# Query transfers of the sliding-window items: whole token tiles of four head pairs, or halves of two

## The reference, cut to what matters

```python
u = _rmsnorm(h, g_pre[i])
qa, ka, va, za, qf, kf, vf, zf, ff, ga, gf = jnp.split(u @ w_in[i], split_idx, axis=-1)
y_swa = _swa_branch(qa, ka, va, sinks[i]) * jax.nn.silu(za)     # 8 query heads, 2 key heads
y_fox = _fox_branch(qf, kf, vf, log_f) * jax.nn.silu(zf)         # 8 heads, causal, 1040 keys
merged = (sigmoid(ga + b) * (y_swa @ w_up_swa[i])
          + sigmoid(gf + b) * (y_fox @ w_up_fox[i]))
h = h + _rmsnorm(merged @ w_out[i], g_post[i])
```

## Time and profile before

| | us |
|---|---|
| median of 3 runs | 817.27 |
| lowest, highest | 816.62, 818.16 |
| profiled execution, device time | 817.68 |
| its span, first to last instruction | 815.9 |

### The profile page before, as it was taken

How to read it: one execution, slowest core, us unless ns; L and a number is a source line. 1 busy time by engine, 2 the same in 40 slices (tenths; PEclk the granted TensorE clock), 3 DMA queues, 4 the chain that set the end, 5 groups by cost and what they waited for, 6 DMA issues and landing times.

```text
span 815.9 us, 12313 instructions
## 1 busy us (share of the span) xinstructions
PE 793.1 (97%) x4270; PEld 638.0 (78%) x4270; DVE 491.9 (60%) x1021; ACT 316.5 (39%) x650; POOL 339.5 (42%) x287
## 2 busy tenths in 40 slices
PE   6999999999999999999999999999998999999996
PEld 4999999988888888888888865656554788878885
DVE  6845788366777867745646466677777644442222
ACT  6532241333334323333333337666767122231111
POOL 1112213454535544444444425758766244412221
PEclk9999999999999999999999999999999999999999
DMA  9342424459855435344344599999700665352222
GB/s 279 105 129 56 131 66 115 126 162 240 205 132 162 109 96 143 110 116 124 102 130 119 137 250 241 243 241 219 184 1 22 208 185 154 104 206 78 103 78 78
DMA packets 127863, 116.05 MB, mean 142 GB/s; under 512 B 29741, under 2 KB 102269, under 8 KB 127802
## 3 DMA queue, kind: packets, MB, share of 16 engines
q1 hardware_dynamic: 126504, 111.53, 51.2%
q10 hardware_dynamic: 1298, 3.74, 1.2%
HBM read 81.99 MB, written 34.96 MB: 143 GB/s over the span
## 4 chain that ended last, share of the span: by engine, by line
PE 79%; DVE 5%; issue 4%; POOL 4%; SPq 3%; DMA 2%; ACT 2%; DVEq 0%; ACTq 0%; POOLq 0%
PE PS L1912 19%; PE PS L1913 19%; PE PS L1914 19%; PE PS L2174 4%; PE PS L2176 4%; PE PS L2175 4%; PE PS L2035 2%; POOL acc L1259 2%; DVE t_val L1648 2%; PE PS L2096 2%; DMA QBs<-q_swa_dram 1%; POOL w_plain L1211 1%; PE PS L2111 1%; PE PS L2127 1%; PE PS L2076 1%
## 5 line engine op out<-in xcount | busy, mean ns | idle before, releaser
L1190 POOL TENSOR_TENSOR ops<-s_sum,ops 128x512 fp32r<-128x512 f32 x64 | 89.1, 1401 | 106.6 <-ACT ops L1288 106.6
L1912 PE MATMUL PS<-t_hi,ops 128*128 128x512 f32 x256 | 100.1, 391 | 0.0
L1914 PE MATMUL PS<-t_hi,ops 128*128 128x512 f32 x256 | 99.9, 390 | 0.0
L1913 PE MATMUL PS<-t_lo,ops 128*128 128x512 f32 x256 | 99.9, 390 | 0.0
L1190 POOL TENSOR_TENSOR ops<-raw,ops 128x512 fp32r<-128x512 f32 x48 | 65.8, 1371 | 64.4 <-ACT ops L1288 64.0
L1211 POOL TENSOR_TENSOR w_plain<-raw,w_plain 128x1024 fp32r<-128x1024 f32 x10 | 27.7, 2769 | 100.7 <-ACT w_plain L1317 100.7
L1259 POOL TENSOR_TENSOR acc<-acc,p_fox 128x400 f32<-128x400 f32 (+5 forms) x76 | 61.4, 828 | 6.9 <-ACT p_fox L1416 5.8
L1730 DVE TENSOR_TENSOR z_tmp<-u,PS 128x512 f32<-128x512 f32 x48 | 33.0, 687 | 45.7 <-PE PS L1914 26.5
L1288 ACT ACTIVATE ops<-s_sum 128x512 fp32r<-128x512 f32 x64 | 39.6, 623 | 52.6 <-DVE s_sum L1524 46.8
L1416 ACT ACTIVATE p_fox<-PS,neg_c_col 128x512 f32<-128x512 f32 (+5 forms) x112 | 54.2, 536 | 13.8 <-PE PS L2082 9.2
L1914 PEld LDWEIGHTS PS<-t_hi,ops 128*128 128x128 f32 x256 | 48.1, 188 | 10.3
(11 more groups left out here) (212 smaller groups left out, 2099.1 us busy)
## 6 DMA issues: line engine op xcount, KB each, us to landing
raw<-in_w_in_dram SPq DMA_DIRECT2D x34, 512.0 KB, 5.2
g_dram<-stage_b SPq DMA_DIRECT2D x32, 256.0 KB, 2.0
tanh_g<-g_dram SPq DMA_DIRECT2D x16, 512.0 KB, 3.9
x_all<-in_x_dram SPq DMA_DIRECT2D x8, 512.0 KB, 7.2
raw<-in_w_in_dram SPq DMA_DIRECT2D x16, 256.0 KB, 4.8
q_dram<-stage_b SPq DMA_DIRECT2D x16, 256.0 KB, 2.4
q_swa_dram<-stage_b SPq DMA_DIRECT2D x16, 256.0 KB, 2.8
z_dram<-stage_b SPq DMA_DIRECT2D x16, 256.0 KB, 2.0
```

The source lines that it names most:

```text
L1190: nc.gpsimd.tensor_tensor(ops[:, i % OPS, 1], op_source(p, name), ops[:, i % OPS, 0].bitcast(F32), ALU.subtract).then_inc(op_ready, 1)
L1912: pe.matmul(dst, hi_w, hi, start=first, stop=False)
L1913: pe.matmul(dst, hi_w, lo, start=False, stop=False)
L1914: return pe.matmul(dst, lo_w, hi, start=False, stop=last)
```

## The change

A tile's queries come in two halves of two head pairs. `load_queries(t, half)` issues three DMAs of 128 KB, in runs of 256 words, on a semaphore of its own for each half of each slot (four in place of two). Half 0 of tile t + 2 is asked for when item 1 of tile t is scored, half 1 when item 3 is. Tiles 0 and 1 are asked for where they were, both halves one after the other. PE waits for the half in which the item's head pair lies.

```diff
-        q_swa_loaded = sems("q_swa_loaded", 2)
+        q_swa_loaded = sems("q_swa_loaded", 4)
...
-            def load_queries(t):
+            def load_queries(t, half):
+                pairs = slice(2 * half, 2 * half + 2)
                 for dst, x in ((QAs[Q0], 0), (QAs[Q1], 0), (QBs[Q0], 1)):
-                    sp.dma_start(dst[:, t % 2].rearrange("r g j q -> r g (j q)").bitcast(F32),
-                                 qsd[x, t].rearrange("(g r) j q -> r g (j q)", g=2)).then_inc(q_swa_loaded[t % 2], 16)
+                    sp.dma_start(dst[:, t % 2, :, pairs, :].rearrange("r g j q -> r g (j q)").bitcast(F32),
+                                 qsd[x, t, :, pairs, :].rearrange("(g r) j q -> r g (j q)", g=2)
+                                 ).then_inc(q_swa_loaded[2 * (t % 2) + half], 16)
...
-                        load_queries(0)
+                        load_queries(0, 0)
+                        load_queries(0, 1)
...
-                load_queries(1)
+                load_queries(1, 0)
+                load_queries(1, 1)
...
-                    elif kind == "score" and st["j"] == PAIRS - 1 and st["t"] + 2 < NQ:
+                    elif kind == "score" and st["j"] % 2 and st["t"] + 2 < NQ:
                         sp.wait_ge(ms_filled, st["ms"] + 1)
-                        load_queries(st["t"] + 2)
+                        load_queries(st["t"] + 2, st["j"] // 2)
...
-                    pe.wait_ge(q_swa_loaded[t % 2], 48 * (t // 2 + 1))
+                    pe.wait_ge(q_swa_loaded[2 * (t % 2) + j // 2], 48 * (t // 2 + 1))
```

To make room for the semaphores, those of the residual's rows in stage D (`again_loaded`) go from one for each of 8 tiles to one for each of 3 slots, with the counts to match; no order and no buffer there changes:

```diff
-        again_loaded = sems("again_loaded", NQ)
+        again_loaded = sems("again_loaded", AGAIN_RING)
...
-                    sp.dma_start(x_again[:, n % AGAIN_RING, :], x_v[n]).then_inc(again_loaded[n], 16)
+                    sp.dma_start(x_again[:, n % AGAIN_RING, :], x_v[n]).then_inc(again_loaded[n % AGAIN_RING], 16)
...
-                    pool.wait_ge(again_loaded[n], 16)
+                    pool.wait_ge(again_loaded[n % AGAIN_RING], 16 * (n // AGAIN_RING + 1))
```

More of the change, by code:

```diff
@@ L1891, in _ @@
                     if n == NQ - 1:
-                        dve.wait_ge(again_loaded[n], 16)
+                        dve.wait_ge(again_loaded[n % AGAIN_RING], 16 * (n // AGAIN_RING + 1))
                         for x in range(2):
```

## The result

| | before | after |
|---|---|---|
| median of 15 runs each, us | 816.72 | 819.84 |
| lowest, highest | 814.96, 819.53 | 817.84, 820.97 |
| profiled execution's span | 815.9 | 818.2 |
| mean granted clock in it | 0.996 | 0.996 |

The ratio is 1.0034, with a 95% interval of 1.0023 to 1.0044: the change makes the kernel 0.34% (about 3 us) slower. The forecast of 817.2 us was wrong, and 819.84 lies above its range, which ended at 818.9.

A forecast was written before the change was run, and what follows sets the result against it. PE was taken as the bound, with the order of bytes in the full DMA queue deciding its waits. −0.67 at item 8 and +0.6 at stage C's start gave −0.07, or 817.2 us from the median 817.27; range 815.8 to 818.9.

The forecast's parts named there:

- What bounds the kernel: Whole kernel: PE is busy 793.1 of 815.9 us, so time is won only where PE stands still.
- The two waits named: PE's 1.3 us wait for queries at item 8 would go; that for `QB<-max_dram` before stage C would grow, 0.7 to 1.3.
- Part 1: Item 8, first of token tile 2: its query wait goes and 0.67 us is kept; bounds 0.67 and 1.45.
- Part 2: Stage C's start: tile 0's three extra issues on SP delay the awaited transfer, +0.6 us; bounds 0 and 1.3.
- twice that: Upper bound of the cost at stage C's start: 1.3 us.
- Parts 3 and 5: Tile 1 and SP's remaining issues, and stage D's semaphores: cost 0 for each.
- Part 4: Unit 19: half 0 of tile 3 goes ahead of pair 1's last values; slack 0.5 us, cost 0.
- The price of smaller runs: DMA engines, runs cut from 2048 to 1024 bytes: −13% to +3% in time for a byte, taken as 0.
- a sign that the prediction named for being wrong: A DMA rate clearly under 241 GB/s in 493 to 526 us.
- A: Item 8 and stage C's start: the gain comes whole, 1.45 us, and the start costs nothing; 815.8 us, chance 0.17.
- B: Unit 19: 1 KB runs, 30% dearer in the full queue, make pair 1's last values late; 819.2 us, chance 0.13.
- C: Item 8: the first half comes no earlier, leaving only the start's cost; 817.9 us, chance 0.15.

The follow-up runs named there:

- e2_only0: Kernel before with only token tile 0 in halves (six DMAs of 128 KB), tiles 1 to 7 whole; 820.82 us, ratio 1.0045.
- e1_whole0: Changed kernel with token tile 0 whole again (three DMAs of 256 KB), tiles 1 to 7 in halves; 815.88 us, ratio 0.9997.
- e3_pad0: Kernel before, all tiles whole, with three tiny DMAs issued right behind tile 0's; 818.8 us, ratio 1.0017.
- e11_whole0: The kernel of e1_whole0 measured a second time, in more rounds; 815.72 us, ratio 0.9984.
- e6_latehalf: Changed kernel with half 1 of tile 0 issued behind FoX pair 0's first transfers, not ahead of them; 816.02 us, ratio 0.9986.
- e10_rows: Changed kernel with tile 0 on one semaphore, in six 128 KB DMAs of one group each, runs of 2 KB; 819.05 us, ratio 1.0017.
- e5_behind0: Changed kernel with tile 0 whole and issued behind FoX pair 0's first transfers, tiles 1 to 7 in halves; 817.04 us, ratio 1.0000.
- e4_poolset: Changed kernel with the clearing of `QBs` moved from DVE to POOL, at about 465 us; 819.06 us, ratio 1.0027.
- e8_fill: Changed kernel with 16 unused matmuls filling PE's wait ahead of unit 0's score; 818.48 us, ratio 1.0021.

## Why the prediction was wrong

**What bounds the kernel: right in kind.** The two waits named were the two that moved, and the start's was the one that mattered. "What counts is the order of the bytes" held for the full queue and not for the nearly empty one at the start.

**Part 1, the gain at item 8: right in size, in part by luck.** Item 8's score follows 0.09 us behind the masks of unit 14 (519.26 and 519.35) and not 1.56. Of that 1.5 us, 0.5 is left at unit 19 (3.95 late became 3.5) where 0.67 was taken. The rest is given back to ACT as its rows said: the wait for `p_fox` is in the list with 1.4 us. But in the changed kernel the first half landed at 518.2 (509.96 + 8.2), later than the whole tile in before; the wait went because PE was late too, and e2_only0 has the same 0.5 us with a whole tile. The proof of the part itself is e1_whole0: its first half landed at 512.9 (506.2 + 6.7), earlier than the 515.2 forecast, and item 8 was scored at 514.77 without a wait.

**Part 2, the cost at stage C's start: the term that failed.** It was +0.6 with bounds 0 to 1.3, and it measured 3.0 here, 2.1 in e2_only0 and 1.3 to 2.1 in the other kernels with six DMAs for tile 0, taken from stage B's last product. SP's time was right (0.65 a DMA, and no less for half the bytes), and so, nearly, was tile 0's own last landing: 471.2 (468.44 + 2.8) against 471.6 forecast and 471.0 before. The step that failed is the next one, that the engines lose only by how much later tile 0 lands. Two things were wrong in it. The shortage of SP's time goes on to what stands behind, and three issues cost 1.1 even where they carry nothing (e3_pad0). And the sum let the transfers behind go at 260 GB/s whatever stood ahead; they ran at 152 to 201 for three microseconds in every kernel with tile 0 in six DMAs of 128 KB. The upper bound "twice that" came from no row. A bound from the whole of SP's 1.95 us plus such a dip (1.8 us of missing bytes, an estimate from after) would have held the result. Why the dip comes stays open.

**The missing term: the clock.** Part 2 said of PE's wait only that it is added. A standstill that grows from 0.7 to 3.7 us is followed by PE at half clock here, and the kernel pays 1.0 us more at stage C's start. No row ahead of the prediction shows a low clock, but the trace of before had one, at stage D (631.5 us above), and the prediction made no use of it. Start and clock together are 4.0 us where 0.6 stood in the sum; less the 0.5 of item 8 that is 3.5, and the medians differ by 3.1.

**Parts 3 and 5: right.** Tiles 1 to 7 in halves cost nothing measurable (e1_whole0, e11_whole0), and stage D shows no wait of the change's.

**Part 4, unit 19's slack: right in this kernel, and thinner than need be.** No wait appeared there. By the bound of Part 4 the values were there by 531.9 (`y` landed at 523.13 + 11.0, less 2.2) and PE came at 532.29: 0.4 us where 0.5 was forecast, with both 3.6 us later. In e1_whole0, where the start isn't late, it is 525.1 (518.8 + 8.5 - 2.2) against 527.72, so 2.6 us.

**The price of smaller runs: 0, right for the queue as a whole.** The rate in 493 to 526 us is 231 GB/s after and 244 in e1_whole0, against 241 before. The 231 is 4% under, in the direction of a sign that the prediction named for being wrong; but the two kernels have the same runs there, so it is no price of runs. The counts came as forecast. DMA packets of before and after:

```profile
DMA packets 127863, 116.05 MB, mean 142 GB/s; under 512 B 29741, under 2 KB 102269, under 8 KB 127802
```

```profile
DMA packets 131320, 116.06 MB, mean 142 GB/s; under 512 B 30125, under 2 KB 108797, under 8 KB 131258
```

These are 3,457 more, and 6,528 more under 2 KB. The Trainium skill, *DMA: Bandwidth & Descriptors*, section "Bandwidth", asks for large batches (its figures are of DMAs issued from GpSimd, these are SP's), and I had set it aside. For tiles 1 to 7, behind a queue of 12 us, the runs agree with setting it aside. For tile 0, issued to a queue that is nearly empty, its direction held: the same bytes in six DMAs cost 1.3 to 3.0 us.

**The rivals.** A (the start costs nothing) is what e1_whole0 gives when tile 0 stays whole. B had the sign and nearly the size, 819.2, but its place, unit 19, and its cause, dear runs, were both wrong. C failed: in e1_whole0 the first half did come earlier (512.9). The rival that was wanted, a start that costs two or three microseconds and lowers the clock, wasn't among them: the side "slower" had been given to a far place with a thin cover, and not to the one wait on the path that the change lengthens for certain.

## What to carry to other kernels

Splitting a DMA is free behind a deep queue and dear in front of a wait: count the issues that stand ahead of the transfer on which the bottleneck waits, at SP's full price for each (0.65 us here), and put behind it what isn't needed first (e6_latehalf: 3.8 us between the medians of two kernels that differ in the place of three issues). A change that asks for things earlier should be made for the tiles whose wait is seen, and not for all of them in one form. Ask, too, what a late start does to a gain further on before adding the two. And where a change makes a standstill of PE several times longer, put a term for the clock behind it, and take its size from a stretch at half clock in the same trace.

## What I had not expected of the hardware

- The issue of a DMA on SP mostly holds it 0.57 to 0.62 us (0.65 from one to the next) for 64 partitions by 2 groups, with 8 KB, 128 KB or 256 KB in it. With one group (64 runs of 2 KB, e10_rows) it is 0.6 but for the first. Some are held longer: one into `QA` 1.24 us, after.
- The transfers of FoX's first keys ran at 152 to 201 GB/s for some 3 us wherever tile 0 stood ahead of them in six DMAs of 128 KB, with the engines busy for 0.72 to 0.93 of the time. Behind three of 256 KB they ran at 245 to 257 (225 with three small ones added). Clearing of `QBs` and run length don't explain it. The rate also drops, earlier, when only three of 128 KB (e6_latehalf, 184 GB/s in 467 to 471 us, share 0.85) or none (e5_behind0, 180, share 0.80) stand ahead, so a short queue at their start may be what these kernels share; that isn't tested by itself, and why the busy engines move less stays open.
- Between kernels that differ in nothing at this place the start varied: 1.3 us late in e4_poolset, 2.1 in e2_only0 and e8_fill, 3.0 in after. Each had one profiled execution, so what part of this is the kernels' own can't be told.
- After a standstill of 3.68 us PE ran at the 1.2 GHz level for about 3.4 us, and so it did behind four of five shorter ones from 1.76 us on. Such a stretch cost 1.0 us at stage C's start, where ACT sets part of the pace in before, and 1.6 us at stage D's, in the execution of before, where PE's products stand back to back; there it came behind a wait of 0.58 us, in 6 of 13 kernels.
